# A two-stream block kernel: the convolution taps of the mixer spread anew over the panels, the queries and the heads

## The reference, cut to what matters

```python
h = rms_norm(x, mix_norm[l])
p = h @ w_in[l]                      # 384 + 256 + 32 + 2*512 columns
attn = mla_group(queries' latent, keys' and values' latent, rope key, ...)   # 8 heads, 96 wide
conv = conv_group(p[..., o_cv:], conv_w[l], conv_b[l], conv_ln_g[l], conv_ln_b[l])
x = x + jnp.concatenate([attn, conv], axis=-1) @ w_out[l]

def conv_group(u_raw, conv_w, conv_b, ln_g, ln_b):
    a, g = u_raw[..., :CONV_W], u_raw[..., CONV_W:]
    u = a * jax.nn.sigmoid(g)
    y = depthwise causal convolution of u, 31 taps, 512 channels
    return jax.nn.silu(layer_norm(y + conv_b, ln_g, ln_b))
```

## Time and profile before

| | |
|---|---|
| runs | 2367.49 us median of 3 (2366.96 to 2367.79) |
| the profiled execution | 2366.76 us |
| its span in the trace | 2365.1 us |
| granted TensorE clock, mean | 0.983 of full speed |
| layer 0's mixer | from 206 us to 361 us (first mixer matmul to ffn2's first) |
| layer 1's mixer | from 751 us to 908 us |

### The profile page before, as it was taken

How to read it: one execution, slowest core, us unless ns; L and a number is a source line. 1 busy time by engine, 2 the same in 40 slices (tenths; PEclk the granted TensorE clock), 3 DMA queues, 4 the chain that set the end, 5 groups by cost and what they waited for, 6 DMA issues and landing times.

```text
span 2365.1 us, 37299 instructions
## 1 busy us (share of the span) xinstructions
PE 2273.4 (96%) x13800; PEld 1972.2 (83%) x13800; DVE 1609.2 (68%) x2710; ACT 1104.0 (47%) x1752; POOL 113.7 (5%) x155
## 2 busy tenths in 40 slices
PE   9999879999999979999999999999999999999998
PEld 8998668998998758998777778888888888888888
DVE  6667657767767757777455545445446898888996
ACT  5443335445443325445555543333434656666664
POOL 0000000000000000211122201011100000000000
PEclk9999979999999979999999999999999999999999
DMA  8654216565565215564344342122221222222222
GB/s 326 229 201 167 72 72 245 197 230 192 209 222 177 85 41 213 198 231 122 81 78 73 73 97 70 64 71 72 72 80 53 99 81 85 83 89 82 87 98 90
DMA packets 83069, 301.88 MB, mean 128 GB/s; under 512 B 10405, under 2 KB 10789, under 8 KB 82469
## 3 DMA queue, kind: packets, MB, share of 16 engines
q1 hardware_dynamic: 78336, 284.72, 34.5%
q0 software_dynamic: 2048, 4.20, 3.0%
q10 hardware_dynamic: 2600, 11.81, 1.4%
HBM read 299.64 MB, written 1.05 MB: 127 GB/s over the span
## 4 chain that ended last, share of the span: by engine, by line
PE 75%; DVE 17%; ACT 4%; issue 3%; DMA 0%; DVEq 0%; ACTq 0%; another core or an unknown queue 0%
PE ps L750 48%; PE ps L798 11%; PE ps L862 4%; DVE wsplit L2192 3%; DVE work L2922 2%; PE ps L1381 2%; DVE work L2934 2%; PE ps L1242 1%; DVE work L2412 1%; PE ps L1105 1%; PE ps L1119 1%; ACT wsplit L1509 1%; PE ps L1095 1%; DVE work L2954 1%; DVE work L2966 1%
## 5 line engine op out<-in xcount | busy, mean ns | idle before, releaser
L750 PE MATMUL ps<-hsplit,wsplit 128*128 128x256 f32 (+1 forms) x8376 | 1379.6, 322 | 27.2 <-DVE wsplit L2192 11.7
L750 PEld LDWEIGHTS ps<-hsplit,wsplit 128*128 128x128 f32 x8376 | 1204.7, 191 | 160.0 <-DVE wsplit L2192 18.4
L2192 DVE TENSOR_TENSOR wsplit<-ring,wsplit 128x1024 fp32r<-128x1024 f32 x465 | 574.6, 1237 | 351.3 <-ACT wsplit L1509 349.6
L1509 ACT ACTIVATE wsplit<-ring 128x1024 fp32r<-128x1024 f32 x463 | 488.4, 1057 | 527.0 <-PE ps L750 395.0
L798 PE MATMUL ps<-wsplit,fsplit 128*128 128x512 f32 x1056 | 256.5, 392 | 1.9 <-DVE fsplit L2326 1.7
L798 PEld LDWEIGHTS ps<-wsplit,fsplit 128*128 128x128 f32 x1056 | 192.6, 188 | 40.1 <-issue 3.3
L2288 DVE SCALAR_TENSOR_TENSOR work<-ring,work 128x1024 f32<-128x1024 f32 x96 | 120.4, 1254 | 1.2 <-DMA ring<-panels 1.1
L2412 DVE SCALAR_TENSOR_TENSOR work<-work,vec 128x256 f32<-128x256 f32 x240 | 108.3, 482 | 4.4
L1589 ACT ACTIVATE work<-ps 128x256 f32<-128x256 f32 x88 | 33.8, 384 | 161.0 <-PE ps L750 161.0
L750 PEld LDWEIGHTS ps<-wsplit,hsplit 128*128 128x128 f32 x768 | 96.4, 199 | 5.3 <-issue 3.8
L862 PE MATMUL ps<-work,ring 128*128 128x256 f32 x416 | 99.9, 387 | 0.0
(11 more groups left out here) (367 smaller groups left out, 2312.0 us busy)
## 6 DMA issues: line engine op xcount, KB each, us to landing
ring<-panels SPq DMA_DIRECT2D x539, 512.0 KB, 4.1
work<-latent_weights ACTq DMA_DIRECT2D x2, 2304.0 KB, 11.8
work<-rpb POOLq DMA_DIRECT2D x64, 64.0 KB, 6.6
work<-conditions ACTq DMA_DIRECT2D x6, 512.0 KB, 5.3
cst<-constants ACTq DMA_DIRECT2D x1, 1408.0 KB
work<-x SPq DMA_DIRECT2D x2, 512.0 KB, 5.1
work<-post_rows ACTq DMA_DIRECT2D x2, 512.0 KB, 3.9
cT<-ctx ACTq DMA_DIRECT2D x1, 1024.0 KB, 6.7
```

Of the source, the lines that this page charges most:

```text
L750: ins = mm(out_, w(a), x(b), start=start and n == 0, stop=stop and n == 2, **kw)
L1509: af(wsplit[:, split_slot(name, n), 0, :], ring[:, slot, :], ACT.Copy).then_inc(high_ready, 1)
L2192: tt(parts[:, 1, :], ring[:, slot, :], parts[:, 0, :].bitcast(fp32), ALU.subtract)\
```

## The change

On TensorE the two panels of group 2 come in front of the three of the queries' latent (the eight rope matmuls that stood between group 2's now stand by themselves behind the latent's last panel). The gate panel of group 3 comes first, in the place where the input panel was; the input panel follows between `turn_heads(0)` and `turn_heads(1)`, into bank 5, with a wait on `head_sq`. The second transposes of `turn_heads(1)` go to bank 0, with a wait on `conv_gate_in`. `scores(1)` waits for `gated(3)`, because bank 5 holds its input. Head 2 and head 1 have 4 fillers in place of 2. `conv_sum` stands in front of head 6's values. On ScalarE `gate(2)` and `gate(3)` come earlier, `high("wout", 1)` and `high("wout", 2)` around `gate(3)` and `heads_in(0)`. On VectorE `gate_in(2)` comes after ten pairs of taps, `gated(2)` after two more; group 1's last taps alternate with group 2's; all of group 2's are done before the first head; two `low` and 10 taps of group 3 stand in front of `maxima(0)`; the heads have 3 taps, 0, 3, 3 and 6, 3, 3 in the order of heads 0 to 5, all of group 3. The panels' order in DRAM follows.

```diff
--- before.py
+++ after.py
@@ -618,6 +618,7 @@
             return per_layer(SEC[name].first, l) + (i * per_round + (n + 1)) + START
         OUT_BANK = (1, 6, 6, 6)
+        TURN_BANKS = ((2, 3, 6, 1), (4, 0, 7, 6))
         FFN_BANKS, MIX_BANKS, LAST_BANKS = (4, 5, 7, 0, 1, 2, 3, 3), (0, 1, 2, 3, 4, 5, 7, 7), (0, 1, 2, 3, 4, 4, 5, 5)
         def h_at(q):
@@ -882,14 +883,16 @@
                     return mm(ps[:, 7, o:o + 1], lat_sq[:, tiles[j], t * 128:(t + 1) * 128], ones[:, 0:1], start=j == 0,
                               stop=j == len(tiles) - 1)
+                pe.wait_ge(conv_u_ready, l * 4 + 1)
+                win(6, 0, 0)
+                win(7, 0, 1)
                 pe.wait_ge(lat_loaded, l * 16 + 16)
-                win(6, 3, 0, between=lambda j: rope(j))
-                win(7, 3, 1, between=lambda j: rope(4 + j))
+                win(8, 3, 0, between=lambda j: rope(j))
+                win(9, 3, 1, between=lambda j: rope(4 + j))
                 pe.wait_ge(lat_ready, l * 2 + 1)
-                win(8, 4, 0, between=lambda j: latent_sum(j // 2, 0, j % 2))
-                pe.wait_ge(conv_u_ready, l * 4 + 1)
-                win(9, 0, 0, between=lambda j: rope(8 + j))
-                win(10, 0, 1, between=lambda j: rope(12 + j))
+                win(10, 4, 0, between=lambda j: latent_sum(j // 2, 0, j % 2))
+                for j in range(8, 16):
+                    rope(j)
                 pe.wait_ge(lat_ready, l * 2 + 2)
                 for t in range(2):
@@ -921,8 +924,10 @@
                 def turn_heads(t):
                     pe.wait_ge(qk_rows, l * 2 + t + 1)
-                    for n, bank in enumerate(((2, 3, 6, 1), (4, 5, 7, 6))[t]):
+                    for n, bank in enumerate(TURN_BANKS[t]):
                         src = (q_n, k_n)[n // 2][t]
+                        if (t, n) == (1, 1):
+                            pe.wait_ge(conv_gate_in, l * 4 + 4)
                         if (t, n) == (0, 3):
                             pe.wait_ge(v_ready, l * 2 + 2)
                         if (t, n) == (1, 3):
@@ -933,9 +938,10 @@
                         last.then_inc(qk_turned, 1)
                 pe.wait_ge(conv_u_ready, l * 4 + 3)
-                win(11, 0, 0)
+                win(11, 0, 1)
                 turn_heads(0)
-                win(12, 0, 1)
+                pe.wait_ge(head_sq, l * 2 + 2)
+                win(12, 5, 0)
                 turn_heads(1)
                 keep_clock(2, 10)
@@ -1000,10 +1006,11 @@
                                (rows_done, l * 12 + 8) if n == KD - 1 else None, ready=ready, tiles=tiles)
                 scores(0)
+                pe.wait_ge(conv_u_ready, l * 4 + 4)
                 scores(1)
                 for h in range(HEADS):
                     if h < 3:
-                        keep_clock(2, 12 if h == 0 else 2)
+                        keep_clock(2, 12 if h == 0 else 4)
                     if h in (4, 6):
                         pe.wait_ge(mix_split_ready, l * 6 + h // 2)
                     transposes(h)
@@ -1011,13 +1018,13 @@
                         scores(h + 2)
                     if h == 2:
                         turn_out(0)
+                    if h == 6:
+                        conv_sum()
                     values(h)
                     if h in (3, 5):
                         wout(h // 2 - 1, (0,))
                         turn_out(h // 2)
                         wout(h // 2 - 1, (1,))
-                    if h == 6:
-                        conv_sum()
                 conv_var()
                 wout(2, (0,))
                 turn_out(3)
@@ -1656,11 +1663,11 @@
                 gate(1)
                 act.wait_ge(panels_used, use_count("win", l, 5))
                 latent((0, 1), 2, V_KVL)
-                act.wait_ge(panels_used, use_count("win", l, 7))
+                gate(2)
+                act.wait_ge(panels_used, use_count("win", l, 9))
                 latent((2, 3), 3, V_QL)
-                act.wait_ge(panels_used, use_count("win", l, 8))
+                act.wait_ge(panels_used, use_count("win", l, 10))
                 latent((4,), 4, V_QL + 2)
-                gate(2)
                 act.wait_ge(lat_ms_done, l + 1)
                 af(tok, ps[:, 7, 0:68], ACT.Copy).then_inc(tok_ready, 1)
@@ -1701,19 +1708,20 @@
                 values_out(0)
                 head_factors(1)
                 values_out(1)
-                for n in range(3):
-                    high("wout", l, n)
+                high("wout", l, 0)
                 def heads_in(t):
-                    for n, bank in enumerate(((2, 3, 6, 1), (4, 5, 7, 6))[t]):
+                    for n, bank in enumerate(TURN_BANKS[t]):
                         act.wait_ge(qk_turned, l * 8 + 4 * t + n + 1)
                         dst, h = (qT, kT)[n // 2], 4 * (n % 2)
                         af(dst[0:QK, h:h + 4, t * 128:(t + 1) * 128], ps[0:QK, bank, :].rearrange("p (h c) -> p h c", h=4),
                            ACT.Copy, scale=gains[0:QK, n // 2:n // 2 + 1]).then_inc(qk_ready, 1)
+                high("wout", l, 1)
+                gate(3)
                 heads_in(0)
-                gate(3)
+                high("wout", l, 2)
                 heads_in(1)
                 def exps(h):
@@ -2391,12 +2399,14 @@
                                  ALU.mult))
                 def gate_in(c):
-                    dve.wait_ge(panels_used, use_count("win", l, (1, 3, 10, 12)[c]))
+                    dve.wait_ge(panels_used, use_count("win", l, (1, 3, 7, 11)[c]))
                     ts(gate_e[:, c, :], ps[:, (0, 1, 0, 0)[c], T:2 * T], SIG_MIN, None, ALU.max).then_inc(conv_gate_in, 1)
                 def gated(c):
                     dve.wait_ge(conv_gate_ready, l * 4 + c + 1)
-                    tt(u_pad[:, c, CONV_K - 1:], ps[:, (0, 1, 0, 0)[c], 0:T], gate_e[:, c, :], ALU.mult).then_inc(conv_u_ready, 1)
+                    if c == 3:
+                        dve.wait_ge(panels_used, use_count("win", l, 12))
+                    tt(u_pad[:, c, CONV_K - 1:], ps[:, (0, 1, 0, 5)[c], 0:T], gate_e[:, c, :], ALU.mult).then_inc(conv_u_ready, 1)
                 last_tap = [0] * 4
@@ -2431,14 +2441,24 @@
                 taps(0, 3)
                 gated(1)
                 taps(0, 1)
-                for j in range(CONV_K):
+                for j in range(10):
                     taps(0, 1)
                     taps(1, 1)
                     if j == 3:
                         ada_out(l, 0)
                 gate_in(2)
+                for j in range(2):
+                    taps(0, 1)
+                    taps(1, 1)
                 gated(2)
-                taps(2, 10)
+                for j in range(CONV_K):
+                    taps(0, 1)
+                    taps(1, 1)
+                    if j > 4:
+                        taps(2, 1)
+                    if next_tap[1] == CONV_K:
+                        break
+                taps(2, 4)
                 dve.wait_ge(tok_ready, l * 2 + 2)
                 V.did(ts(q_bias, tok[:, 65:68:2], EPS / Q_LORA, EPS * EPS, ALU.mult, ALU.add))
@@ -2486,11 +2506,12 @@
                 taps(2, 2)
                 turned_heads(1)
                 wide = lambda v, n: v.unsqueeze(1).to_broadcast([128, n, T])
-                taps(2, 6)
                 gate_in(3)
-                taps(2, 2)
+                taps(2, CONV_K)
+                low("wout", l, 0)
                 gated(3)
-                low("wout", l, 0)
+                low("wout", l, 1)
+                taps(3, 10)
                 def maxima(h):
                     b = 4 + h % 2
@@ -2514,12 +2535,12 @@
                         maxima(h + 2)
                     if h == 2:
                         out_low(0)
-                    if h < 2:
-                        low("wout", l, h + 1)
-                    for _ in range(6):
-                        taps(2, 1)
-                        taps(3, 1)
-                    if h == 7:
+                    if h == 1:
+                        low("wout", l, 2)
+                    elif h < 5:
+                        taps(3, 3)
+                    if h == 6:
+                        taps(3, CONV_K)
                         dve.wait_ge(conv_sum_done, l + 1)
                         stt(gate_x, wide(ps[:, 4, 0:T], 4), -1.0 / CONV_W, acc[:, :, :], ALU.mult, ALU.add)\
                             .then_inc(conv_centred, 1)
@@ -2533,7 +2554,11 @@
                            ps[:, 7, 0:T].rearrange("p (t h c) -> p t h c", t=2, h=2),
                            rsum[:, :, 2 * j:2 * j + 2].unsqueeze(3).to_broadcast([128, 2, 2, 64]), ALU.mult).then_inc(attn_ready, 1)
                     if h in (3, 5):
+                        taps(3, 2)
                         out_low(h // 2)
+                        taps(3, 4)
+                        if h == 5:
+                            taps(3, CONV_K)
                         low("wout", l, h // 2 + 2)
                 out_low(3)
                 dve.wait_ge(conv_rstd_ready, l + 1)
```

(2 more changed lines are left out.)

## The result

The changed kernel takes 2332.19 us (median of 4 runs, 2327.00 to 2332.73) against 2367.64 for the kernel before (4 runs beside it, 2366.96 to 2368.70): ratio 0.9845, 95% interval 0.9828 to 0.9862, a gain of 35.4 us, or 1.5%. The forecast was 2330. The profiled execution took 2332.28, with a span of 2330.6; the spans differ by 34.5.

The account below looks back on a forecast made before the run. VectorE's order sets the pace in the mixers' heads, and TensorE's waits cost clock. Gains of 18.5, 1.7 and 22.0 make 42.2 us, less a 4.4 clock fall 37.8: from 2366.76 to about 2330 us, range 2321 to 2348.

Parts of the forecast that it names:

- The chain to the first head: Layer 0 before the heads: group 2's gate at 233.9, scores(0) at 278.6, first maximum 283.1, first copy 285.3.
- The heads at full clock: Both mixers without clock falls: 18.5 us to layer 0's variance, 1.7 behind it, 22.0 in layer 1, sum 42.2.
- one fall of 4.4 in one of the two layers: Clock loss assumed in the heads, as if falling at head 4 and staying for heads 4 and 5: 4.4 us.
- the ledger: Full-clock times forecast step by step through layer 0's heads, from scores(0) at 278.6 to the variance at 314.6.
- the 1.7 that I had booked as a gain: Layer 0 from the variance to the next feed-forward: 28.3 us down to 26.6.
- The second rival: Clock low through most of the heads, half on the chain: 22 of 42.2 us lost, 2347; chance 0.22.
- The values' waits: TensorE's values waiting for VectorE's copies of the probabilities: total down from 13.1 us to some 5.
- The clock in the heads: Granted TensorE clock in the heads: over 0.85 if right, under 0.75 if wrong.
- a tail of over 28: Stretch after the variance: longer than 28 us would show the prediction wrong.
- Group 3's side: Turning of the heads: reordered panels and gate(3) remove a 1.62 us wait; scores(0) 3.1 us earlier, gated(3) at 276.9.

Follow-up runs that it names:

- e3: Changed kernel with 20 fillers instead of 12 before head 0's transposes and 8 added before head 4's values; 2325.34 us.
- e7: Kernel before with only fillers added in TensorE's waits behind the transposes of heads 1, 3, 4, 5 and 6; 2358.81 us, ratio 0.9962.
- e8: Kernel before with only VectorE's new order of taps and splits, TensorE, ScalarE and panels untouched; 2352.87 us, ratio 0.9938.
- e6: Kernel before with only the sum over the channels moved in front of the seventh head's values; 2360.14 us, ratio 0.9971.
- e9: Changed kernel with group 3's panel order, banks, gate and second transposes put back, without the added waits; 2331.61 us.
- e11: e5 with transposes in place of its fillers; four runs took 2315.7 to 2317.7 us.
- e4: Changed kernel with group 3's taps dealt out anew (4 before the first maximum, not 10) and 8 fillers before head 0; 2324.45 us.
- e5: Changed kernel with taps dealt out as in e4, plus fillers before the values of heads 4, 6 and 7; 2317.08 us, ratio 0.9785.
- e1: Changed kernel with group 2's panels late again, gate(2) and the taps of groups 0 to 2 as before; 2339.61 us, ratio 0.9873.
- e2: Changed kernel with the sum over the channels put back behind the seventh head's values; 2341.87 us.

## Why the prediction was right, point by point

**The chain to the first head** was right to 0.2 us: gate of group 2 at 233.93 with a wait of 2.77 (233.9, 2.6), the norms' end as before, scores(0) at 278.48 (278.6), the first maximum at 282.92 (283.1), the first copy at 285.26 (285.3). No wait appeared at 248.6, at `gated(3)` or at the sum.

**The heads at full clock** were right: 42.2 us was the sum, and e3, whose clock is 1.00 in both mixers but for one stretch, has the second feed-forward of layer 1 42.4 us earlier than before (908.25 to 865.85, in the fastest of its runs). e7 and e8 show parts of it: clock alone 9.1, VectorE's order alone 12.9 at a clock that still fell. With the sum alone at 5.2 (e6), the parts don't add up to a whole, since each moves the clock.

**The clock was the term that was mis-sized.** I took "one fall of 4.4 in one of the two layers". There were three low stretches in each. In layer 0 they are from about 285 to 291, after the wait of 1.90, from 305 to 312, after the wait of 2.11, and from 319 to 322, at the variance, where the waits in front were 0.88 and 0.65. In layer 1 they are from 817 to 821, 834 to 841 and 848 to 851, after the same waits. From scores(0) to the variance it took 40.4 us in layer 0 and 39.4 in layer 1, for 36.0 in the ledger (314.6 less 278.6): 4.4 and 3.4. Behind the variance, 28.3 instead of 26.6 in layer 0, so the 1.7 that I had booked as a gain did not come, and 28.0 in layer 1, 1.4 lost. Together 10.9, against 10.5 by the measured 31.7 of 42.2, and not 4.4. The median still came within 2.2 us of the forecast because 2.8 us of the profiled gain lay in the second block, where the change does nothing: that closeness is luck. The second rival (a clock low through most of the heads, 22 us lost) had the right kind of loss and twice its size.

**The values' waits** fell to 4.7 (some 5 foretold). The clock in the heads was foretold as over 0.85; it was 0.86 in layer 1 and 0.83 in layer 0. Behind the variance layer 0 took 28.3 us, and the prediction had named a tail of over 28 as a sign of being wrong: that sign came, by 0.3, and it is the clock's: e3 took 26.6 there at 1.00.

**Group 3's side** moves the first maximum by the 2.0 us a layer that I expected of e9, and yet the changed kernel is no faster for it. It lengthens TensorE's wait before head 0, which I had seen (1.95) without a price on what lengthened it; that this is the reason fits the two profiles and isn't shown beyond them.

**The transposes.** The prediction weighed a rule of the Trainium skill ("TensorE: Matmul & The Clock Gate", Part 4: PE-mode transpose), by which transposes don't count as work for the clock. e11 speaks against it for the fp32 transposes of this kernel: in the wait of layer 1 behind which the clock fell in e4, they held it at 1.00 as the matmuls of e5 did, and the four runs took 2315.7 to 2317.7 us, for 2316.2 to 2317.8 in e5 and 2323.2 to 2326.3 in e4. The same page of the Trainium skill says, in "Why this matters for your kernels", that gaps without matmuls bring the clock down; e3 and e7 agree, by 1.00 in the heads and 0.96 of granted clock with gaps filled; in e7 the clock fell in both layers behind a wait of 3.78 that was left. The page speaks of longer gaps than the waits of 1.90 and 2.11 us behind which the clock fell in the changed kernel.

What stays open: why the clock falls behind a wait in one place and not behind the same wait in another. e1 (2.38 and 2.39), e2 (1.90 and 1.89) and e4 (2.10 and 2.11) each have such a pair, kept at 1.00 in layer 0 and fallen in layer 1. The same kernel gave 2327.0 once and 2332.1 to 2332.7 three times, and there is a profile of only one of these.

## What to carry to other kernels

When one engine's side work stands in front of a copy that another engine waits for, count per handshake, not in total: with the same 124 taps a layer, the two layers together took 12.9 us less when some of the taps were moved ahead of the heads, and a split with them (e8), and the changed kernel took a further 15 us less when its taps were put into waits that VectorE had anyway and TensorE's waits were filled (e5: 2317.08 against 2332.19, faster than both kernels). An edit's worth on the chain and its effect on TensorE's longest wait must be priced together: fillers belong into the waits that stay, as many as end just before the wait does. And a part's worth is read at the start of the stage behind it: here the totals of single profiles moved by up to 5.8 us for stretches that no edit touched.

## What the runs showed of the hardware that I had not expected

In the changed kernel the granted clock came down to 0.50 behind waits of 1.90 and 2.11 us between busy stretches, in both layers; in e9 it stayed up behind waits of 1.19 and 0.52. But the length of the wait didn't decide it: in layer 0 the clock also stayed up behind 1.90 (e2), 2.10 (e4) and 2.38 (e1). Transposes kept the clock at 1.00 (e11). And the clock falls in a stretch of the second block in every kernel of this study, by different lengths (the clock was low for some 4 us of 40 in the changed kernel and for some 14 in e4), so that two profiles can differ by almost 6 us where their instructions are the same.
